# The first 256 expert slots gathered apart, with contiguous factors, and one expert's weights fetched ahead of w_out

## The reference, cut to what matters

```python
merged = (gate[:, :, 0] * (o_dn.astype(x.dtype) @ w_branch_dn)
          + gate[:, :, 1] * (o_sb.astype(x.dtype) @ w_branch_sb))
return merged @ w_out
...
h = layer_norm(DEEPNORM_ALPHA * h + mix, ln1_g[i], ln1_b[i])
...
for gi in range(N_GROUPS):
    hid = (jax.nn.silu(jnp.einsum("td,edf->tef", t, expert_w_gate[gi]))
           * jnp.einsum("td,edf->tef", t, expert_w_up[gi]))
    hid = hid * combine[:, gi, :, None].astype(hid.dtype)
    y = y + jnp.einsum("tef,efd->td", hid, expert_w_down[gi])
```

## Time and profile before

| | us |
|---|---|
| median of 3 runs | 827.79 (827.59 to 828.42) |
| the profiled execution | 826.47 |
| its span | 824.6 |
| PE busy in the span | 768.2 (93%) |
| DVE, ACT busy | 484.2 (59%), 373.7 (45%) |

### The profile page before, as it was taken

One profiled execution on the slowest core, in us unless ns is written; L12 is line 12 of the kernel. 1 busy time (PEld: TensorE's weight loads), 2 busy tenths in 40 slices (PEclk: granted clock), 3 DMA queues, 4 the chain that ended last, 5 costly groups with the idle time before them and its releaser, 6 DMA issues.

```text
span 824.6 us, 16208 instructions
## 1 busy us (share of the span) xinstructions
PE 768.2 (93%) x6678; PEld 645.2 (78%) x6678; DVE 484.2 (59%) x838; ACT 373.7 (45%) x568; POOL 54.8 (7%) x94
## 2 busy tenths in 40 slices
PE   8999999999999999999999999999999977677675
PEld 6999998999999998999998999899954533344342
DVE  4555667767676678867854355387774533323325
ACT  4555764554544556567454554474331211111113
POOL 2200041000000000110101000000000000000000
PEclk9999999999999999999999999999999989879889
DMA  9954362655556554544352233449989999999993
GB/s 309 301 194 138 118 178 91 203 173 183 194 166 200 192 169 151 176 132 153 103 155 67 91 103 103 152 155 372 421 330 422 420 419 421 420 422 420 422 419 145
DMA packets 89027, 193.82 MB, mean 235 GB/s; under 512 B 3630, under 2 KB 69521, under 8 KB 76546
## 3 DMA queue, kind: packets, MB, share of 16 engines
q1 hardware_dynamic: 86640, 186.66, 61.8%
q0 software_dynamic: 1888, 4.61, 1.8%
q10 hardware_dynamic: 434, 1.62, 0.5%
HBM read 191.83 MB, written 1.05 MB: 234 GB/s over the span
## 4 chain that ended last, share of the span: by engine, by line
PE 71%; DMA 17%; DVE 6%; ACT 2%; issue 1%; SPq 1%; DVEq 0%; ACTq 0%
DMA expert_w<-in_expert_w_up 16%; PE PG L2026 15%; PE PG L2028 14%; PE PG L2027 14%; PE PG L2635 3%; PE PM L2026 3%; PE PM L2028 3%; PE PM L2027 3%; PE PM L2486 1%; ACT whi L851 1%; SPq L677 1%; PE PM L2665 1%; DMA raw<-in_moba_w_qkv 1%; PE PG L2657 1%; PE PM L2111 1%
## 5 line engine op out<-in xcount | busy, mean ns | idle before, releaser
L2026 PE MATMUL PG<-hT_hi,whi 128*128 128x256 f32 (+1 forms) x816 | 235.5, 289 | 1.1 <-DVE hT_lo L1372 1.1
L2028 PE MATMUL PG<-hT_hi,wlo 128*128 128x256 f32 (+1 forms) x816 | 230.5, 282 | 0.0
L2027 PE MATMUL PG<-hT_lo,whi 128*128 128x256 f32 (+1 forms) x816 | 230.4, 282 | 0.0
L1354 DVE TENSOR_TENSOR wlo<-raw,whi 128x2048 fp32r<-128x2048 f32 x73 | 167.2, 2291 | 66.7 <-ACT whi L851 66.5
L2026 PEld LDWEIGHTS PG<-hT_hi,whi 128*128 128x128 f32 x816 | 153.9, 189 | 7.3 <-issue 4.1
L2028 PEld LDWEIGHTS PG<-hT_hi,wlo 128*128 128x128 f32 x816 | 154.1, 189 | 0.0
L2027 PEld LDWEIGHTS PG<-hT_lo,whi 128*128 128x128 f32 x816 | 153.5, 188 | 0.2
L851 ACT ACTIVATE whi<-raw 128x2048 fp32r<-128x2048 f32 x73 | 139.4, 1910 | 22.3 <-PE PG L2028 20.0
L2635 PE MATMUL PG<-expert_w,xw 128*32 128x256 f32 x992 | 73.2, 445 | 34.8 <-DMA expert_w<-in_expert_w_up 34.8
L2635 PEld LDWEIGHTS PG<-expert_w,xw 128*32 128x32 f32 x992 | 35.9, 124 | 57.3 <-issue 45.3
L1939 DVE SCALAR_TENSOR_TENSOR y_lo<-PG,small,y_hi 128x512 fp32r<-128x512 f32 x16 | 12.0, 750 | 94.1 <-ACT y_hi L1281 94.1
(11 more groups left out here) (525 smaller groups left out, 1334.5 us busy)
## 6 DMA issues: line engine op xcount, KB each, us to landing
expert_w<-in_expert_w_gate SPq DMA_DIRECT2D x32, 1024.0 KB, 26.7
expert_w<-in_expert_w_up SPq DMA_DIRECT2D x32, 1024.0 KB, 26.5
expert_w<-in_expert_w_down SPq DMA_DIRECT2D x32, 1024.0 KB, 26.8
raw<-in_ffn_w_up SPq DMA_DIRECT2D x22, 1024.0 KB, 5.1
raw<-in_w_in SPq DMA_DIRECT2D x22, 1024.0 KB, 5.3
raw<-in_moba_w_qkv SPq DMA_DIRECT2D x12, 1024.0 KB, 5.5
raw<-in_ffn_w_down SPq DMA_DIRECT2D x11, 1024.0 KB, 4.9
raw<-in_moba_w_o SPq DMA_DIRECT2D x4, 1024.0 KB, 5.3
```

What stands on the lines that cost most here:

```text
L1354: dve.tensor_tensor(lo_of(n), raw[:, n % R, :], hi_of(n).bitcast(F32), ALU.subtract).then_inc(s_lo, 1)
L2026: pe.matmul(dst, lh, rh, start=start, stop=False, **kw)
L2027: pe.matmul(dst, lh, rl, start=False, stop=False, **kw)
L2028: return pe.matmul(dst, ll, rh, start=False, stop=stop, **kw)
```

## The change

Four things change.

- The places of expert 0's gate and up become those of the delta net's `kd`, `vtok` and what lies behind them; expert 2's take the former ones. SP issues expert 0's two loads before the four granules of `w_out`, once ACT has taken `O 2` out of PSUM. Expert 5's up moves behind expert 6's gate and up in SP's queue.
- `X_hi` and `X_lo` are laid out by feature group (`[P, KD, P]`), so that the weights of the gather are contiguous words; ACT and DVE read X at every eighth word to write them (`by_feature`).
- The gather is made in two parts: slots 0 to 255 (`FIRST`) of all eight groups, two groups to a bank, and then slots 256 to 511 in four pieces `rest_of_slots(b)` of two groups, which PE does between the first two experts. `pick` is made in halves, the second behind the counts. ACT takes out k = 0, 1, 4, 5, DVE k = 2, 3, 6, 7, first all first halves, then the second ones.
- PE's order of the first experts is written out: expert 1's gate and up come before expert 0's transposes, from a window of its own `xw_second`; `rows_of_tokens` and with it ACT's `rows_out` come later; `add_tokens` moves from expert 5 to 9; `add_of` waits for `s_back` too.

```diff
-        RING_SLOT = [[0, 1, 4], [2, 3, 15], [5, 6, 9], [7, 8, 14], [10, 11, 17], [13, 12, 16]]
+        RING_SLOT = [[5, 6, 4], [2, 3, 15], [0, 1, 9], [7, 8, 14], [10, 11, 17], [13, 12, 16]]
...
+            return X[:, t, :].rearrange("p (n k) -> p k n", k=KD)
...
+            consumed(sp, "O", 2)
+            for kind in range(2):
+                expert_load(0, kind, 0)
...
-            sp.wait_ge(s_xga, KD // 2)
-            sp.wait_ge(s_xgv, KD // 2)
-            expert_load(5, 1, 5)
             for e in range(NU, NE):
                 sp.wait_ge(s_guse, 2 * (e - NU) + 2)
                 for kind in range(2):
                     expert_load(e, kind, e % NU)
+                if e == NU:
+                    sp.wait_ge(s_xga, KD)
+                    sp.wait_ge(s_xgv, KD)
+                    expert_load(NU - 1, 1, NU - 1)
...
-                act.activation(X_hi[t][:, :], X[:, t, :], ACT.Copy).then_inc(s_xhi3, 1)
+                act.activation(X_hi[t][:, :, :], by_feature(t), ACT.Copy).then_inc(s_xhi3, 1)
...
-                dve.tensor_tensor(X_lo[t][:, :], X[:, t, :], X_hi[t][:, :].bitcast(F32), ALU.subtract).then_inc(s_xlo, 1)
+                dve.tensor_tensor(X_lo[t][:, :, :], by_feature(t), X_hi[t][:, :, :].bitcast(F32), ALU.subtract).then_inc(s_xlo, 1)
...
+                rest_of_slots(0)
+                gate_up(0, pair[:, :, 0:WIN], 0, 1, True, True)
+                rest_of_slots(1)
+                rest_of_slots(2)
+                pe.wait_ge(s_win, 1)
+                gate_up(1, xw_second, 1, 1, True)
+                rest_of_slots(3)
+                pe.wait_ge(s_gu, 1)
+                transposes(0)
+                rows_of_tokens()
+                down(0)
```

More of the change, by code:

```diff
@@ L1264, in _, with features_in @@
             act.preload_act_table_set("exp_and_others")
[L1265 to L1269, removed]
+            def features_in(k, c, src, count):
+                act.wait_ge(s_xg, count)
+                act.activation(pair[:, k, c], src, ACT.Identity, scale=lncol[:, 2, k:k + 1], bias=lncol[:, 3, k:k + 1]).then_inc(s_xga, 1)
+            for k in filter(by_scalar, range(KD)):
+                features_in(k, slice(0, FIRST), first_slots(k), k // 2 + 1)
+            for k in filter(by_scalar, range(KD)):
+                features_in(k, slice(FIRST, PAIRS), other_slots(k), KH + k // 2 + 1)
+                if k == 1:
                     act.wait_ge(s_scalar, 1)
@@ L1864, in _, with picks @@
             step(dve.tensor_reduce(pos, of_two, AX.X, ALU.add))
+            def picks(t, c):
+                step(dve.tensor_scalar(pick2[:, t, c], con("slots")[:, c], pos[:, 1, t, :], None, ALU.is_equal))
+                dve.scalar_tensor_tensor(pick[:, t, c], con("slots")[:, c], pos[:, 0, t, :], pick2[:, t, c], ALU.is_equal, ALU.add).then_inc(s_P, 1)
             for t in range(TT):
-                step(dve.tensor_scalar(pick2[:, t, :], con("slots"), pos[:, 1, t, :], None, ALU.is_equal))
-                dve.scalar_tensor_tensor(pick[:, t, :], con("slots"), pos[:, 0, t, :], pick2[:, t, :], ALU.is_equal, ALU.add).then_inc(s_P, 1)
+                picks(t, slice(0, FIRST))
             rows_lo(1)
@@ L1874, in _, with features_out @@
             dve.tensor_copy(offi[0:1, NE:NE + 1], cmax[0:1, :]).then_inc(s_off, 1)
+            for t in range(TT):
+                picks(t, slice(FIRST, PAIRS))
+            def features_out(k, c, src, count):
+                dve.wait_ge(s_xg, count)
+                dve.tensor_scalar(pair[:, k, c], src, lncol[:, 2, k:k + 1], lncol[:, 3, k:k + 1], ALU.mult, ALU.add).then_inc(s_xgv, 1)
+            for k in (2, 3, 6, 7):
+                features_out(k, slice(0, FIRST), first_slots(k), k // 2 + 1)
             each = [P, SEQ // WIN, NE]
@@ L2600, in _, with features_of @@
             keep_warm(3, con("ident"), con("ident"))
-            def features_of_slots(k, t, parts=range(2)):
-                for i in parts:
-                    mine = (X_hi, X_lo)[i][t][:, :].rearrange("p (n k) -> p k n", k=KD)[:, k, :]
-                    mm = pe.matmul(PM[:, k % 4, :], mine, pick[:, t, :], start=t + i == 0, stop=t + i == 2)
-                    if t + i == 2:
-                        mm.then_inc(s_xg, 1)
+            def features_of(k, t, i, c, dst, start, done):
+                mm = pe.matmul(dst, (X_hi, X_lo)[i][t][:, k, :], pick[:, t, c], start=start, stop=t + i == 2, skip_group_check=True)
+                if done:
+                    mm.then_inc(s_xg, 1)
             for t in range(TT):
```

101 lines of the change are left out of this document (57 added, 44 removed).

## The result

| | before | after |
|---|---|---|
| median, us (8 runs each) | 827.38 (826.60 to 828.42) | 830.13 (829.39 to 835.01) |
| ratio, 95% interval | 1 | 1.0040 (1.0027 to 1.0053) |
| span of the profiled execution, us | 824.6 | 828.1 |

The changed kernel is slower, by 2.8 us of the medians (3.3 by the ratio); the forecast was 826.8 and its range ended at 829.0.

A forecast was written before the change was run, and what follows sets the result against it. From 560 us the remaining expert transfers and the holes between them set the end. Shift = max(T0, T51 - 4.98) - 604.39: -2.8 without surcharge, -1.0 with it; 827.79 - 1.0 = 826.8 us, range 824.8 to 829.0.

The forecast's parts named there:

- the hole: Memory nearly idle from 602 us, full rate from 606.5, because SP issued the seventeenth load only at 604.39.
- T51: SP's issue of expert 5's up, which waits for all features; forecast 608.4 us, with 4.98 us covered by two loads.
- T0: SP's issue of expert 6's gate, which waits for expert 0's gate and up on PE; forecast 602.7 us.
- the small gap behind expert 6's up: In memory traffic near 609 us: a small new hole of 0.8 us, as expert 5's up is issued late.
- The early loads: Expert 0's gate and up ahead of w_out: its first granule might land 2 us later, hidden, cost 0.
- The gather without surcharge: Gather in halves with X reads at no extra cost: T0 600.8, T51 606.6, shift of the end -2.8 us.
- The surcharge: ACT and DVE reading X at every eighth word: +0.78 us per X_hi, +0.90 per X_lo, in all 1.8 us.
- 1.43 us is lost for everything behind: Tile 0: X_hi0 0.78 later, X_lo0 0.90 longer, 0.25 idle on DVE; 1.43 us lost up to the picks.
- The dearer hop: Rival at X_hi0, X_lo0, X_lo1: twice the surcharge, T51 611.0, shift +1.6 us, 829.4 us; chance 0.17.
- The second hole behind the late diagonals: Rival: late diagonals hold up down of expert 0; a 4 us slip costs 1.7, about 828.5 us; chance 0.08.

The follow-up runs named there:

- the kernel with pairs: Changed kernel with X_hi and X_lo laid out by pairs of adjacent features instead of single features; 824.87 us, ratio 0.9969 to the kernel before.
- the clock held: Changed kernel plus seven more warming matmul calls on PE ahead of tile 1's transposes; 828.06 us, ratio 1.0007 to the kernel before.

## Why the prediction was wrong

**What bounds the kernel, and the form of the sum** were right. The end hangs on the first loads after the hole; T51 decided and not T0; the small gap behind expert 6's up is there (172 GB/s from 612 to 614). (By its own terms T0 adds up to 602.6, not 602.7, which changes nothing.)

**The early loads** were hidden, and worth nothing: w_out's split starts at 552.44 for 552.48, and the kernel without them is as fast.

**The gather without surcharge** was right to 0.2 us in both issue times, as the kernel with pairs shows.

**The surcharge** was right in its mechanism and nearly in its size. X_lo was put at 2.12 and took 2.22 and 2.10 us. X_hi was put at 1.84 and took 2.11 and 2.09: PE's factor of 1.74 was too low for ACT, which paid 2.0, and near for DVE's 1.7 to 1.8. (No run takes ACT's part and DVE's apart; by their durations tile 0's 1.8 us is 1.05 and 0.99, less the 0.25 that DVE was idle.) The forecast's two estimates for X_lo, +0.69 and +1.48 us, lie to either side of the 0.99 and 0.88 measured. The step "1.43 us is lost for everything behind" should have had 1.82, 0.4 us more. At the second picks and between the two issues another 0.2 and 0.5 us came on top.

**The step that failed** is "From there DVE is the chain up to the picks, so 1.43 us is lost for everything behind". The forecast moved DVE's chain as a block and left PE's side of the same stretch as it was. But PE feeds that chain twice, with the logits and with the counts, and had 2.25 us of warming matmuls between them that just fitted. While DVE was late, PE had no matmul for 1.6 us, its clock fell to the 1.2 GHz level, and the warming matmuls, which had been filler, became the longest piece of the chain: 4.05 us. With the slower logits that is 2.4 us of the 3.5 us by which T51 was missed (608.4 forecast, 611.90 measured). The forecast held PE's time in that stretch for fixed and never listed it: the earlier trace rows show five weight loads of a later group of `keep_warm`, at 592.85, but not the eighteen at 588.72, and the name says what these matmuls are there for.

**The rivals.** The dearer hop gave 829.4, near the result, but by luck and not by its mechanism: it doubled both surcharges (+1.8 and +1.56 us), and the passes took 0.9 to 1.05 us more. With the passes as they really are and the clock held, the changed kernel is level with the one before (1.0007). The second hole behind the late diagonals was dismissed on margins of 2.3 us. In the changed kernel it did not come: the matmuls behind the diagonals ran at full clock (1.98 us), and no window from 618 to 632 is under 401 GB/s. In four other profiles it came, those in which both the matmuls behind the diagonals and the first add ran slow.

## What to carry to other kernels

A delay on one engine's chain is also an idle stretch on the engine that waits for it: look in the timeline for what PE does in that stretch, and price what stands behind it at the 1.2 GHz level as well. Where a matmul reads its weights with a step, halving its columns is only worth it if the weight load fits under them; where the data has to be laid out for that, keep pairs of words together, which here cost the writing engines at most 0.09 us a pass and PE 5 to 8 ns a weight load. And once a hole is closed, list the waits behind it again with their new margins.

## What the runs showed of the hardware

- A pass of 1024 elements that reads one fp32 source at every eighth word: ACT 2.08 to 2.13 us for 1.06, DVE (two sources, only one of them hopping) 2.10 to 2.22 for 1.22. In runs of two words: 1.14 and 1.22.
- PE's load of 128x128 fp32 weights: 188 to 192 ns contiguous, 195 or 196 at a step of two words (the gather's), 329 to 339 at a step of eight. Beside 512 columns the last is all but hidden (0.24 us a matmul); beside 256 it sets the pace, 0.24 us for each matmul instead of 0.12.
- The granted clock fell in all three kernels in which PE idled 1.6 to 1.7 us at 587, and in none of the others there. In the kernel before with the contiguous factors it fell again behind 1.26 us at 605. But behind a wait of 2.0 us for the diagonals it read 0.50 in the first profile with pairs (610 to 612) and 1.00 in the second (608 to 612) and in the changed kernel (612 to 614). What decides between the two isn't settled here; it is likely part of the 4 us between runs of one kernel.
